# Down weights of pairs 3 to 5 through four homes outside the ring, and the packed gather behind pair 1's ups

## What is computed

```python
def hier_moe_2(xn, wg, bg, we, be, w_gate, w_up, w_down):
    """Group top-1 then within-group top-2 over SwiGLU experts; exact sparse dispatch."""
    g_prob = jax.nn.softmax((xt @ wg + bg).astype(f32), axis=-1)
    g_top_p, g_top_i = lax.top_k(g_prob, 1)
    ...
    top_val, top_idx = lax.top_k(e_logits, MOE_TOP_K)
    weights = g_top_p * jax.nn.softmax(top_val, axis=-1)
    expert_id = grp[:, None] * MOE_EXPERTS_PER_GROUP + top_idx
```

## Time and profile before

| | before |
|---|---|
| time, median of 3 runs | 992.19 us (991.69 to 995.52) |
| the profiled execution: time, span | 991.52 us, 989.8 us |
| PE busy | 919.8 us (93%) |
| DVE, ACT busy | 307.0 us, 207.3 us |
| moved by DMA | 339.80 MB, 343 GB/s over the span |
| mean granted TensorE clock | 0.990 |
| the opening of the second layer's experts starts | 534.0 us |

### The profile page before, as it was taken

The page is one execution under the profiler, slowest core; times in us unless marked ns, Lnnn a source line. Parts: engine busy times, 40 slices in busy tenths (PEclk is TensorE's granted clock), DMA queues, the critical chain, the costliest instruction groups (busy, mean ns, idle before and its releaser), DMA issues.

```text
span 989.8 us, 11796 instructions
## 1 busy us (share of the span) xinstructions
PE 919.8 (93%) x4653; PEld 493.9 (50%) x4653; DVE 307.0 (31%) x664; ACT 207.3 (21%) x440; POOL 23.3 (2%) x61
## 2 busy tenths in 40 slices
PE   8999999999999998999999999998888888889886
PEld 5777475555655555866447433333333333333332
DVE  3356366333332334132126132222111122101213
ACT  3232353221121114024323021111011111011112
POOL 4001300000000000000000000000000000000000
PEclk9999999999999998999999999999999999999998
DMA  9950546999999999635456999999999999999994
GB/s 318 388 175 4 209 149 248 422 422 421 419 421 420 421 420 387 245 137 170 154 209 232 396 413 380 401 426 430 426 431 427 430 428 427 431 425 427 420 420 201
DMA packets 53970, 339.80 MB, mean 343 GB/s; under 512 B 9917, under 2 KB 10961, under 8 KB 24610
## 3 DMA queue, kind: packets, MB, share of 16 engines
q1 hardware_dynamic: 48048, 337.59, 84.1%
q10 hardware_dynamic: 5458, 1.39, 0.6%
q0 software_dynamic: 416, 0.16, 0.1%
HBM read 338.07 MB, written 1.05 MB: 343 GB/s over the span
## 4 chain that ended last, share of the span: by engine, by line
PE 69%; DMA 22%; DVE 5%; ACT 1%; issue 1%; SPq 0%; DVEq 0%; ACTq 0%
PE ps L1156 23%; PE ps L1220 12%; DMA ring<-in_expert_w_down_dram 11%; DMA ring<-in_expert_w_gate_dram 9%; PE ps L2269 8%; PE ps L2418 5%; PE ps L1239 4%; PE ps L2483 4%; DMA ring<-in_w_up_dram 2%; PE ps L2257 1%; PE ps L1062 1%; PE ps L1579 1%; PE ps L1381 1%; PE ps L1194 1%; PE ps L2393 1%
## 5 line engine op out<-in xcount | busy, mean ns | idle before, releaser
L1156 PE MATMUL ps<-ring,work 128*64 128x256 f32 (+1 forms) x2040 | 339.1, 486 | 20.7 <-DMA ring<-in_expert_w_up_dram 10.5
L1156 PEld LDWEIGHTS ps<-ring,work 128*64 128x64 f32 x2040 | 153.0, 137 | 199.0 <-issue 162.9
L1220 PE MATMUL ps<-ring,work 128*64 128x512 f32 x696 | 159.6, 602 | 9.2 <-DMA ring<-in_expert_w_down_dram 8.0
L913 DVE TENSOR_TENSOR work<-work,ps 128x256 f32<-128x256 f32 (+1 forms) x30 | 16.4, 545 | 273.5 <-PE ps L1156 273.5
L1220 PEld LDWEIGHTS ps<-ring,work 128*64 128x64 f32 x696 | 52.0, 138 | 96.9 <-issue 86.1
L2269 PE MATMUL ps<-xT,ring 128*128 128x256 f32 (+1 forms) x384 | 86.0, 382 | 0.0
L1239 PE MATMUL ps<-parts 128*128 128x512 f32 x248 | 73.7, 419 | 6.6 <-DVE parts L934 6.6
L2269 PEld LDWEIGHTS ps<-xT,ring 128*128 128x128 f32 x384 | 72.3, 191 | 11.3 <-issue 1.2
L1239 PEld LDWEIGHTS ps<-parts 128*128 128x128 f32 x248 | 41.9, 189 | 41.8 <-DVE parts L934 18.5
L741 ACT ACTIVATE work<-ps,small 128x512 f32<-128x512 f32 x30 | 20.6, 687 | 188.4 <-PE ps L1220 188.4
L2418 PE MATMUL ps<-ring,work 128*128 128x512 f32 x128 | 56.0, 595 | 2.2 <-ACT work L1905 1.8
(11 more groups left out here) (392 smaller groups left out, 687.2 us busy)
## 6 DMA issues: line engine op xcount, KB each, us to landing
ring<-in_expert_w_gate_dram SPq DMA_DIRECT2D x20, 2048.0 KB, 17.1
ring<-in_expert_w_up_dram SPq DMA_DIRECT2D x20, 2048.0 KB, 17.6
ring<-in_expert_w_down_dram SPq DMA_DIRECT2D x20, 2048.0 KB, 17.7
ring<-in_w_gate_dram SPq DMA_DIRECT2D x32, 1024.0 KB, 17.4
ring<-in_w_up_dram SPq DMA_DIRECT2D x32, 1024.0 KB, 18.9
ring<-in_w_down_dram SPq DMA_DIRECT2D x32, 1024.0 KB, 16.3
ring<-in_expert_w_up_dram SPq DMA_DIRECT2D x24, 1024.0 KB, 12.6
ring<-in_expert_w_gate_dram SPq DMA_DIRECT2D x23, 1024.0 KB, 11.9
```

Source lines behind the costliest of these rows:

```text
L1156: mm = pe.matmul(ps[CAP * e:CAP * e + CAP, 4 + which, 0:ff], slots, chunks[e][:, k, :], start=(k0 + k == 0), stop=(k0 + k == KC - 1), skip ...
L1220: mm = pe.matmul(ps[CAP * e:CAP * e + CAP, 6 + half, :], hT[:, c0 + k, CAP * e:CAP * e + CAP], columns(chunks[e], k, half), start=(c0 + k ...
```

## The change

1. *The opening.* All eight groups of the packed gather run behind the ups of pair 1 (before, four stood between the ups of pair 0 and the gates of pair 1). The turned hidden of pair 0 now stands between gates and ups of pair 1. Groups 4 and 5 use banks 4 and 5, 6 and 7 use banks 0 and 1.
2. *Homes.* The downs of pairs 3, 4 and 5 use four homes in turn: `aside0`, `aside2`, `aside1`, and a new one, `late`, in `work`, which is free once the gather is through. SP loads (3, 11) into `late`, with a wait for the gather, ahead of pair 2's second up chunk. The other eleven are issued on ScalarE's queue, by `load_again`, once the downs that lay in the home before have been read.
3. *Written out.* Pairs 4 and 5 stand in the code one by one on SP, ACT, DVE and PE, since their downs are no longer in the ring. Their gates and ups stay loads of two chunks.

```diff
-        GATHER_BANKS = {"m1": (6, 0, 1, 2, 3, 5, 6, 0), "m2": (0, 1, 2, 3, 0, 1, 2, 3)}
-        GATHER_ORDER = {"m1": (0, 1, 2, 3, 4, 5, 6, 7), "m2": (0, 1, 2, 3, 4, 6, 5, 7)}
+        GATHER_BANKS = {"m1": (6, 0, 1, 2, 3, 5, 6, 0), "m2": (0, 1, 2, 3, 4, 5, 0, 1)}
+        GATHER_ORDER = {"m1": (0, 1, 2, 3, 4, 5, 6, 7), "m2": (0, 1, 2, 3, 4, 5, 6, 7)}
...
+        LAST_ASIDE = 5
+        for p in range(3, LAST_ASIDE + 1):
+            for j, name in zip(range(8, 12), ("aside0", "aside2", "aside1", "late")):
+                ASIDE["m2"][p, j] = name
...
+                 "late": work[:, 15360:15360 + CH]}
...
-        ASIDE_LAST = ((0, 3), (0, 11), (2, 11))
+        ASIDE_LAST = ((0, 3), (0, 11)) + tuple((p, j) for p in range(2, LAST_ASIDE + 1) for j in (9, 10, 11))
...
-                 "m2": ((0, 1), (2, 1), (4, PAIRS // 2 - 3))}
+                 "m2": ((0, 1), (2, 1), (4, 1), (6, PAIRS // 2 - 4))}
...
+            def load_late(cfg):
+
+                sp.wait_ge(ev("gathered"), 2 * KC)
+                load_whole_aside(cfg, "late")
...
+                        if p0 >= WHOLE[tag]:
+                            for p in (p0, p0 + 1):
+                                wholes = whole_weights(cfg["gate"], cfg["up"], cfg["down"], cfg["ff"], p)
+                                for w in range(4):
+                                    load_whole(place_in_stream(cfg, p, 2 * w), wholes[w], 0, 0, 3 - w % 2)
+                            continue
...
+                            if tag == "m2" and place == cfg["base"] + RING + 15:
+                                load_late(cfg)
...
+            def load_again(freed, *chunks):
+
+                act.wait_ge(ev("aside_used"), 1 + ASIDE_LAST.index(freed))
+                for p, j in chunks:
+                    src, shape = pair_chunks(cfg["gate"], cfg["up"], cfg["down"], ff, p)[j]
+                    name = ASIDE[tag][p, j]
+                    act.dma_start(aside[name].rearrange("p (a b) -> p a b", b=shape[1]), src).then_inc(ev(name), 16)
...
                 take_turned_hidden(n, sfx)
+                if tag == "m2" and isinstance(m, int) and 2 <= m < LAST_ASIDE:
+                    load_again((m, 9), (m + 1, 8), (m + 1, 9))
+                    load_again((m, 10), (m + 1, 10))
+                    if m > 2:
+                        load_again((m, 11), (m + 1, 11))
...
-                gather_rest((0, 1))
-                turn_hidden(n)
-                gather_rest((2, 3))
-                gates_and_ups(getter(1, 0), chunk_used, n + 1, 1, pair=1)
-                gather_rest((4, 6, 5, 7))
+                pe.wait_ge(ev("sil"), n + 1)
+                gates_and_ups(getter(1, 0), chunk_used, n + 1, 1, pair=1, between=lambda: turn_hidden(n))
+                gather_rest(range(KC))
                 turn_weights(n)
...
-                turns = (LAST_A - 4) // 2 - 1
+                for p in (4, 5):
+                    spaced_pair(p, p, 0, EARLIER[tag] + p)
+                turns = (LAST_A - 6) // 2 - 1
```

More of the change, by code:

```diff
@@ L154, in two_block_kernel @@
             "shared_in": ("gain0_in", 16), "shared_down_in": ("pos_in", 32),
-            "aside0": ("x_in0", 16), "aside1": ("x_in1", 16), "aside2": ("meta_in", 32), "aside3": ("gain0_in", 32), "aside_pieces0": ("pos_in", 48), "aside_pieces1": ("pos_in", 112), "gain_spread": ("router_pe", 4), "gain_ready": ("sh_sil", 2),
+            "aside0": ("x_in0", 16), "aside1": ("x_in1", 16), "aside2": ("meta_in", 32), "aside3": ("gain0_in", 32), "aside_pieces0": ("pos_in", 48), "aside_pieces1": ("pos_in", 112), "late": ("pos_in", 176), "gain_spread": ("router_pe", 4), "gain_ready": ("sh_sil", 2),
             "shared_up_in": ("meta_in", 16),
@@ L401, in two_block_kernel, with use_of @@
                         "aside_pieces1": ((from_one[:, :], tables[:, :]), (early_rows[:, :], y[:, 512:1024]))}
-        ASIDE_LAST = ((0, 3), (0, 11), (2, 11))
+        ASIDE_LAST = ((0, 3), (0, 11)) + tuple((p, j) for p in range(2, LAST_ASIDE + 1) for j in (9, 10, 11))
+        def use_of(pair, j):
+            name = ASIDE["m2"][pair, j]
+            return [c for c in sorted(ASIDE["m2"]) if ASIDE["m2"][c] == name].index((pair, j)) + 1
         LAST_A, LAST_B = PAIRS - 2, PAIRS - 1
@@ L446, in two_block_kernel @@
         WHOLE = {"m1": PAIRS, "m2": 4}
-        WHOLE_LAPS = LAST_A - WHOLE["m2"]
         def landings(place):
-            skipped = WHOLE_LAPS if place >= moes[1]["tail"] and place % RING % 2 else 0
-            return 16 * (place // RING + 1 - skipped)
+            whole = range(place_in_stream(moes[1], WHOLE["m2"], 0), moes[1]["tail"])
+            earlier = range(place % RING, place + 1, RING)
+            return 16 * len([q for q in earlier if q % 2 == 0 or q not in whole])
         two = moes[0]["next"]
@@ L694, in products_done @@
             if is_aside(cfg, n, j - 1):
-                return ev("aside_used"), 1 + [c for c in ASIDE[cfg["tag"]] if c in ASIDE_LAST].index((n, j - 1))
+                return ev("aside_used"), 1 + ASIDE_LAST.index((n, j - 1))
             if isinstance(n, int):
@@ L745, in opening @@
                 take_gates(0)
-                take_gathered(1)
                 take_turned_hidden(n)
-                take_gathered(3)
                 take_gates(1)
-                take_gathered(5)
-                take_gathered(7)
+                for f in range(1, KC, 2):
+                    take_gathered(f)
                 take_down(0)
@@ L964, in opening @@
                 hidden(n, 0)
-                take_gathered(0)
-                take_gathered(2)
                 hidden(n + 1, 1)
-                take_gathered(4)
-                take_gathered(6)
+                for f in range(0, KC, 2):
+                    take_gathered(f)
                 take_scatter(n)
@@ L974, in opening @@
                 take_y(n + 1)
-            alone = SHARED_UP + 1 if tag == "m1" else 4
+            alone = SHARED_UP + 1 if tag == "m1" else LAST_ASIDE + 1
             if tag == "m2":
@@ L1086, in gather_rest @@
                 for f in groups:
-                    if f >= 4:
-                        pe.wait_ge(ev("xgP_odd" if f % 2 else "xgP_even"), 4 * turn_ + (f - 4) // 2 + 1)
+                    if f >= 6:
+                        pe.wait_ge(ev("xgP_odd" if f % 2 else "xgP_even"), 4 * turn_ + 1)
+                    elif f >= 4:
+                        pe.wait_ge(ev("h"), EARLIER[tag] + 2)
                     else:
@@ L1247, in get @@
                     views = []
-                    if pair >= WHOLE[tag]:
+                    if pair >= WHOLE[tag] and not is_aside(cfg, pair, j):
                         for e in range(2):
@@ L1261, in get @@
                                 continue
-                            pe.wait_ge(*nth(name, 16))
+                            pe.wait_ge(*nth(name, 16 * use_of(pair, j + e)))
                             views.append(aside[name].rearrange("p (a b) -> p a b", b=shape[1]))
@@ L1348, in moe_tensor @@
                 two_pairs(1, 1, 0, False)
-                turns = (LAST_A - 4) // 2 - 1
+                for p in (4, 5):
+                    spaced_pair(p, p, 0, EARLIER[tag] + p)
+                turns = (LAST_A - 6) // 2 - 1
                 with pe.Fori(0, turns) as i:
                     for odd in range(2):
-                        spaced_pair(None, 4 + odd, i, i * 2 + (EARLIER[tag] + 4 + odd))
+                        spaced_pair(None, 6 + odd, i, i * 2 + (EARLIER[tag] + 6 + odd))
                 for odd in range(2):
-                    p = 4 + 2 * turns + odd
-                    spaced_pair(p, 4 + odd, turns, EARLIER[tag] + p)
+                    p = 6 + 2 * turns + odd
+                    spaced_pair(p, 6 + odd, turns, EARLIER[tag] + p)
             else:
```

2 lines of the change are left out of this document (1 added, 1 removed).

## The result

The changed kernel takes 994.48 us (median of 20 runs, 992.40 to 999.20), the kernel before 991.98 in the same sessions: ratio 1.0029, 95% interval 1.0020 to 1.0038. It is slower by 2.5 us, where 1.5 us less than before was forecast. The profiled execution took 995.94 us, with a span of 994.1.

What follows compares the result with a forecast made beforehand. The weights' DMA stream was taken to bound the second layer's experts: -5.5 for holes filled, +0.3 for smaller loads, +3.7 for a new hole, sum -1.5 us from 992.2, so 990.7 us, range 986.0 to 994.5.

Steps and rivals of the forecast that it cites:

- number 6: Pairs 4 and 5 of the second layer, written out: the same instructions as the loop's, cost 0.
- Steps 1 to 4: Second layer's experts: gather moved -0.75, late home -0.69, homes reloaded for pair 3 -4.07, smaller loads +0.28 us.
- the holes of 5.5 us: Weights' stream sinking below its rate at 556:562 (0.75 us), 584:588 (0.69) and 614:622 (4.07); all to be filled.
- step 3: Pair 3's homes: ScalarE issues three chunks, 7.4 us of transfer, into the 614 hole, with about 2 us to spare: -4.07.
- The sinking at 544:550: Another 0.85 us lost by the stream at 544:550 us, paced by pair 0, forecast to stay.
- Step 5: Eleven DMA issues on ScalarE, 0.3 to 0.5 us each: cost 0; without cover up to 1 us a pair.
- The rival of a long hold: ScalarE held by its own issue from 635.3 us; 30 us would give about 996 us; 3 in 100.
- The share by packets: Queues alternate by packet, not bytes: ScalarE's homes' loads get a third, 143 GB/s, beside SP's double loads from pair 4 on.
- the wait at pair 4: PE waits 5.6 us for the homes' loads of pair 4's second downs, ending pair 4 at 666.9.
- the new hole: Stream stands still from 703.4 to 707.1 us, before pair 7's gates load: +3.7 us.
- full gain: Rival: shares near equal in bytes or homes' loads in time, no new hole, -5.2 us, 987.0 us; 27 in 100.
- Doesn't do what it says, net 0: Rival: the holes come back elsewhere, net 0, 992.2 us; 8 in 100.

Runs made afterwards that it cites:

- before_written_out: The kernel before with only pairs 4 and 5 of the second layer written out, no new home, old gather order: 994.77 us, ratio 1.0034.
- written_out_code_moved: before_written_out with PE's idle products made fewer and wider, leaving 110 instructions to the border at the tail: 991.96 us, ratio 0.9997.
- after_idle_wide: The changed kernel with PE's idle products made fewer and wider, leaving 110 instructions at the tail in place of 14: 991.75 us, ratio 0.9997.
- homes_two_queues: after_idle_wide with half of the homes' loads issued by GpSimd in place of ScalarE, double loads kept: 988.23 us, ratio 0.9966.
- after_code_moved: The changed kernel with 18 one-column products (72 instructions) added on TensorE at 382 us, shifting the code behind them: 998.03 us, ratio 1.0046.
- homes_to_pair3: after_idle_wide with the homes used by pair 3 only, pairs 4 and 5 still written out: 991.24 us, ratio 0.9997.
- homes_to_pair4: after_idle_wide with the homes used by pairs 3 and 4 only, pair 5's downs through the ring: 994.51 us, ratio 1.0027.
- before_code_moved: The kernel before with idle products made fewer and wider, 96 instructions less, leaving 44 at the tail: 992.28 us, ratio 1.0004.

## Why the prediction was wrong

- **The step that failed** is number 6, "Written-out pairs 4 and 5. The same instructions as the loop's: 0". They are the same work, but not in the same place. TensorE ran out of instructions in the tail and stood 3.8 us until the next block came. before_written_out: +3.0 us with this step alone; written_out_code_moved: -2.8 with only the place mended; the changed kernel against after_idle_wide: the same 2.7. Dose by dose, instructions left against the stand: 14: 3.83 and 3.77 us, 10: 3.86, 44: 1.1, 106 and more: none. The packet itself comes in every kernel, with a stand or without, 3.7 to 4.0 us after the last scatter ahead of the branch (932.29 in the changed kernel, 932.59 in the kernel before, 931.82 in after_idle_wide): only what PE still has to do until then differs. That entering a block starts the fetch of the next fits all of them and is argued, not shown.
- **Why only 2.7 us of a larger stand.** 3.83 us and the slower clock: from the first record of the tail to the next row (L1229) it took 21.79 us in the changed kernel and 14.82 in after_idle_wide, 7.0 more. Part was slack: without the stand PE waits 1.27 and 0.87 us for loads later in the tail, with it not at all. 7.0 - 2.1 = 4.9 us is what it cost this execution, which was 1.5 us above the median; executions differ in how long the clock stays low. It was 6.8 us here and 3.4 us in before_written_out, where the same stretch took 20.38 us against 14.81 in the kernel before, 5.6 more.
- **"A microsecond in which the stream stands still after it starts for good is a microsecond of the end"** holds only while the stream is the bound to its end. The tail's slack was 2.07 us in the kernel before (PE waits of 1.32 and 0.75), and I did not read it: any stand of PE there beyond it counts.
- **Steps 1 to 4, the holes of 5.5 us:** right in what they do to the stream. The holes at 556, 584 and 614 are gone; homes_two_queues, where nothing is given back, is 3.4 us faster. Wrong in step 3 is that the three loads would have 7.4 us of free engines: issued at 608.5 and 611.9 us as forecast, they shared with SyncE's queue (84 packets to 75, 33% to 66% of the engines from 616 to 620 us), the last landed at about 634 in place of 631 at the latest, and PE waited 2.1 us for it at pair 3's last downs. The sinking at 544:550, forecast to stay, stayed in after_idle_wide (356 GB/s) and homes_two_queues (378), not in the changed kernel's execution (416). Of the forecast 5.2 us, 5.1 are still there at 720 us in homes_two_queues (168 us at 425 GB/s in place of 412); the last down load lands 3.4 us sooner, at 963.11. Where the other 1.7 go is open; rates differ by under 1% there.
- **Step 5, issues on ScalarE:** right, 11 of 0.33 to 0.45 us, none with a cost that the trace shows. The rival of a long hold did not occur.
- **The share by packets, and the new hole:** right in kind, the central choice. 157 packets to 152; the wait at pair 4 is 6.1 us for 5.6; the hole begins near 703 and has 4.9 us for 3.7. Missed: the clock falls around the end of that wait (0.53 and 0.61 from 664 to 672 us), which makes PE later still; and pair 5's downs, forecast to wait 3.4 us, do not wait, since PE came to them later. So the hole is near its forecast by a chain that is right in one of its two waits. Net of the stream: -5.5 + 0.3 + 4.9 = -0.3 us, as after_idle_wide measured (to about 0.9 us either way).
- **The rivals:** full gain needed equal shares; they came with the split over two queues, not by themselves. "Doesn't do what it says, net 0" is nearest to the stream's part. The loss itself was in none of them.

The Trainium skill's "Runtime: NRT & Kernel Launch", section "Instruction fetch mechanics", says that instructions come in 16 KiB blocks of 256, that prefetch is sequential, that a taken branch to a target outside the two pages held forces a fetch first, and that crossing a border is mostly hidden. The trace agrees with the blocks (35 packets of 16 KB for 9146 instructions, the skipped code included), and not with the last where a border follows a branch closely: 3.8 us. What it says of the branch no run here tests: some of the target's own block was there, since eight records ran. The same section says that kernels prefer full unrolling where possible; here unrolling two pairs cost 3.0 us, by its length alone.

## What to carry to other kernels

- An edit that changes an engine's instruction count moves all code behind it. Before crediting or blaming the edit itself, look for "issue" idle of several us with an instruction packet in it, and run a control whose work is the same and whose code is shifted. A median moved by 0.3% here with no change in the work.
- After a taken branch over skipped code leave some 60 TensorE instructions or more to the next border where the DMA engines are full. That is an estimate from 6.4 us at 0.11 us each; between 44 (1.1 us) and 106 (nothing) no run lies, and none has such a branch with the engines idle. Put no padding of quick instructions over a border.
- Queues share by packets. A load that must get past a stream of big packets needs packets as big, or a second queue; making the stream's packets smaller buys the share with some of the stream's rate (421 in place of 427 GB/s).

## What the runs showed of the hardware

- With the DMA engines full, the next instruction block was in use 6.4 us after the last scatter ahead of the branch, in the changed kernel (928.45 to 934.87), 6.3 us in before_written_out (926.90 + 1.20 to 934.44) and 6.0 us at the other branch, in after_code_moved (383.18 to 389.18). The packet itself took 1.1 us.
- TensorE's loop over the pairs, some 450 instructions with two borders in them, made its turns from 749 us until it ended (about 872) with no instruction packet on queue 8; the next came at 901. In the kernel before there was none from 679 to 890 us. A loop of that length stays on the engine.
- In all these kernels, from 381 us on, each idle stretch of PE of 3.5 to 7.4 us had 3.4 to 10.2 us at half clock (1.2 GHz) that began in it or just behind it. Of the six of 1.9 to 2.4 us two had (2.11 us in homes_to_pair3 and 2.35 in homes_to_pair4); the 1.1 us of before_code_moved's tail had not.
- GpSimd's loads of 1 MB, in its software queue, took 0.53 to 0.58 us to issue each and got as many packets as ScalarE's (174 to 175).
